# Scores of two differential heads as one group of four row groups in a fused two-layer transformer trunk

## The chip, the cores and the metric

One Trainium2 chip, one of its cores. The metric is the device time of one execution in microseconds (us). TensorE (PE in the rows) multiplies matrices, its weight loads stand in rows of their own (PEld), VectorE is DVE, ScalarE is ACT, GpSimd is POOL, and SyncE (SP) issues the loads of weights. Each engine works through its own queue of instructions in order, and engines wait for each other at semaphores.

## The reference

Two layers over 256 tokens of width 1024, all in float32. A layer normalizes x, makes queries, keys and values for 16 heads of width 64 with one projection, runs three kinds of attention side by side, projects back, adds attention over a memory, and ends with a gated feed-forward part. The change touches the four *differential* heads. Each has two softmaxes with queries and keys of width 32 and one set of values:

```
s1 = q1 @ k1.T * 32**-0.5          # 256 x 256, causal mask
s2 = q2 @ k2.T * 32**-0.5
p  = softmax(s1) - lam * softmax(s2)
o  = p @ v
```

The other twelve heads (six with a dilated mask, six causal) have one softmax each, with queries and keys of width 64. So a layer has 20 softmaxes, numbered n = 0 to 19: 0 to 7 belong to the differential heads (two to a head), 8 to 19 to the others.

## The kernel before

**Float32 as three products.** A weight unit (128 x 2048) is loaded into `raw`, ACT rounds it into `whi` (`split_hi`, L636 or L638) and DVE takes the difference into `wlo` (`split_lo`, L961 or L963). TensorE multiplies hi by hi, hi by lo and lo by hi. Units go round a ring of three buffers, and SP loads the next unit of a buffer when both splits of the last one are done. Units 0 to 11 of a layer are the q/k/v projection, 12 and 13 the key/value projection of the memory (`mkv`).

**Places.** In the first half of a layer all engines follow one counter g, the *place*. At each place TensorE runs one *filler*: four 512-column matmuls of the projections (L1581), which need nothing from the attention. The attention is put between the fillers by tables at the end of the file: what stands at place g in a table is issued ahead of filler g by TensorE, and at place g in the order of the loops by ACT (L773 to L824) and DVE (L1245 to L1292). The order of every queue is fixed by these tables; nothing is decided at run time.

**One pair of softmaxes** (`duo` d, softmaxes 2d and 2d+1) goes through these steps:

- `score(d)` on TensorE (L1702 to L1711): for the two halves of the queries, one matmul per softmax. A differential softmax uses 32 rows of the array (rows 0, 32, 64 or 96 upwards, as `SOFTMAXES` gives it); the two matmuls of a pair use different rows and write to different PSUM banks (`n % 2`, so banks 0 and 1). It waits until the maxima of the previous pair are taken, since those read the same banks.
- `mask_max(n)` on DVE (L1163 to L1180): adds the mask, writes the scores from PSUM to one of four buffers `prob`, and takes the row maxima (`nm`).
- `exps(n)` on ACT (L728 to L735), then `combine(h)` on DVE (L1182 to L1193), which puts the two softmaxes of differential head h together.
- `transpose_p(m)` on TensorE (L1713 to L1731), `probT_out(m)` on ACT (L737 to L741), `weigh_v(m)` on TensorE (L1733 to L1747), the product with the values.

**The second half of the keys.** `transpose_qk(2)` on TensorE (L1658 to L1675) transposes the keys of heads 8 to 15 into banks 3 and 4. ACT copies bank 3 (`qkT_out(2)`, L720) and DVE copies bank 4 (`qkT_out(2)`, L1159) into `kT`. Since `weigh_v(0)` writes its results into banks 3 and 4 too, it waits for both copies (`qkT_first` and `qkT_second`, L1737 and L1738).

**The other waits that matter here.** `split_lo` of a unit waits for its `split_hi`; `chunk_out(i, t)` on ACT (L687 to L697) takes a finished projection block out of PSUM.

Of the kernel before, what the change touches and what calls it, by code (L numbers as in the profile page):

```python
# [42 lines left out]
DIFF, DIL, MOBA = 4, 6, 6  # L43
# [34 lines left out]
NS = len(SOFTMAXES)  # L78
# [22 lines left out]
def trunk(nc, x, mem, w, gains, consts, out):  # L101
    with ExitStack() as ctx:
# [25 lines left out]
        prob = [sq[:, 512 * b:512 * b + 512] for b in range(4)]  # L128
# [36 lines left out]
        masks = table[:, 0:6 * P].rearrange("p (c n) -> p c n", c=2)  # L165
# [34 lines left out]
        ps = ctx.enter_context(nc.psum_tensor("ps", [P, 8, 512], F32))  # L200
# [72 lines left out]
        scores = signal("scores", DUOS)  # L273
        nmax = signal("nmax", NS)
# [335 lines left out]
        def _(act):  # L610
# [58 lines left out]
            for layer in range(DEPTH):  # L669
# [38 lines left out]
                def qkT_out(e):  # L708

                    act.wait_ge(qkT_ps.sem, qkT_ps.at(layer, 2 * e + 1))  # L710
                    dst, j = (kT, qT)[e % 2], 4 * (e // 2)
                    bank = QKT_BANKS[e][0]
                    if e % 2:
# [9 lines left out]
                    if layer == 0 and e == 1:  # L723
                        act.wait_ge(qkT_ps.sem, qkT_ps.at(layer, 2 * e + 2))
                        act.activation(qT[:, 2:4, :].rearrange("p k n -> p (k n)"), ps[:, QKT_BANKS[1][1], :], ACT.Copy)\
                           .then_inc(qkT_second.sem, 1)
# [46 lines left out]
                for g in range(6, LAST + 1):  # L773
# [10 lines left out]
                    for m in range(HEADS):  # L784
                        if g == T_AT[m]:
                            probT_out(m)
                    for e in range(4):
                        if g == QKT_AT[e]:
                            qkT_out(e)
                    for d in range(DUOS):  # L790
                        for b in range(2):
                            if g == S_AT[d] + EXPS_AFTER[d][b]:
                                exps(2 * d + b)
# [151 lines left out]
        def _(dve):  # L945
# [116 lines left out]
            for layer in range(DEPTH):  # L1062

                if layer == 0:
# [5 lines left out]
                    for k in range(4):  # L1070
# [7 lines left out]
                        ins = dve.tensor_tensor(wlo[0][:, cols], raw[0][:, cols], whi[0][:, cols].bitcast(F32), ALU.subtract)  # L1078
# [84 lines left out]
                def mask_max(n):  # L1163

                    head, _, rows = SOFTMAXES[n]
                    kind = 1 if DIFF <= head < DIFF + DIL else 0
                    if n % 2 == 0:
                        dve.wait_ge(scores.sem, scores.at(layer, n // 2 + 1))
                    if layer == n == 0:
                        dve.wait_ge(s_table.sem, 16)  # L1170
                        dve.wait_ge(s_memss.sem, 1)
                    if n >= 4:

                        dve.wait_ge(pT_ps.sem, pT_ps.at(layer, SOFTMAXES[n - 4][0] + 1))
                    for t, (a, b) in enumerate(((0, P), (P, 3 * P))):
                        scale = -float(rows) ** -0.5 if kind else q_root[:, t, n:n + 1]
                        ins = dve.tensor_tensor_reduce(prob[n % 4][:, a:b], ps[:, n % 2, a:b], masks[:, kind, a:b],  # L1177
                                                       scale, -3.0 * NEG, ALU.add, ALU.min,
                                                       nm[:, n, t:t + 1])
                    ins.then_inc(nmax.sem, 1)  # L1180
# [64 lines left out]
                for g in range(6, LAST + 1):  # L1245
# [3 lines left out]
                    for d in range(DUOS):  # L1249
                        if g == S_AT[d]:  # L1250
                            mask_max(2 * d)
                            mask_max(2 * d + 1)
                        if d < DIFF and g == S_AT[d] + COMBINE_AFTER[d]:
                            combine(d)
                    for e in range(4):
                        if g == QKT_DVE_AT[layer][e]:
                            qkT_out(e)
# [149 lines left out]
                for t in range(T):  # L1407
                    ins = dve.tensor_scalar(rs_diag[:, t * P:(t + 1) * P], ident, rs[:, 1, t:t + 1], None, ALU.mult)
# [83 lines left out]
        def _(pe):  # L1492
# [50 lines left out]
            for layer in range(DEPTH):  # L1543
# [114 lines left out]
                def transpose_qk(e):  # L1658

                    if e % 2:  # L1660
                        pe.wait_ge(roped.sem, roped.at(layer, e // 2 + 1))
                    else:
                        pe.wait_ge(roped_keys.sem, roped_keys.at(layer, e // 2 + 1))
                    part, half = 1 - e % 2, e // 2
                    if layer == 0 and e < 2:
                        pe.wait_ge(m_lo.sem, (2, 4)[e])
                    for b in range(2):
                        if e == 3 and b == 0:
                            pe.wait_ge(nmax.sem, nmax.at(layer, 2 * HALF_DUO))
                        for j in range(2):  # L1670
                            for t in range(T):
                                a = j * SEQ + t * P
                                c = part * D + (4 * half + 2 * b + j) * P
                                ins = pe.transpose(ps[:, QKT_BANKS[e][b], a:a + P], qkv[:, t, c:c + P], ident)
                        ins.then_inc(qkT_ps.sem, 1)  # L1675
# [23 lines left out]
                                           mem_sb[:, t, (4 * h + k) * P:(4 * h + k + 1) * P], ident)  # L1699
                    ins.then_inc(m_ps.sem, 1)  # L1700

                def score(d):  # L1702

                    if d:
                        pe.wait_ge(nmax.sem, nmax.at(layer, 2 * d))
                    for qa, qb, kb, a in ((0, P, P, 0), (P, 2 * P, 2 * P, P)):
                        for n in (2 * d, 2 * d + 1):
                            h, base, rows = SOFTMAXES[n]
                            q, k = qT[base:base + rows, h // 2, qa:qb], kT[base:base + rows, h // 2, 0:kb]
                            ins = pe.matmul(ps[:, n % 2, a:a + kb], q, k, start=True, stop=True)  # L1710
                    ins.then_inc(scores.sem, 1)  # L1711

                def transpose_p(m):  # L1713
                    n = 2 * m if m < DIFF else m + DIFF
# [56 lines left out]
                for g in range(LAST + 1):  # L1771
                    for n in range(2, 4):
                        if layer == 0 and g == FIRST_AT[n - 2]:
                            build_x(0, X_MIX, FIRST_ORDER[n])
                    if layer and g == 3:
                        for q in range(2, 4):
                            build_x(layer, X_MIX, q)
                    for q in range(4):
                        if layer == 0 and g == MEM_AT[q]:
                            build_mem(q)  # L1780
                    for m in range(DIFF):
                        if g == V_AT[m]:
                            weigh_v(m)
                    for m in range(DIFF, HEADS, 2):
                        if g == V_AT[m + 1]:
                            weigh_v_duo(m)
                    for d in range(DUOS):
                        if g == SCORES_AT[d]:
                            if d == 0:
                                pe.wait_ge(qkT_first.sem, qkT_first.at(layer, 2))  # L1790
                                pe.wait_ge(qkT_second.sem, qkT_second.at(layer, 2))
                            if d == HALF_DUO:
                                pe.wait_ge(qkT_first.sem, qkT_first.at(layer, 4))
                                pe.wait_ge(qkT_second.sem, qkT_second.at(layer, 4))
                            score(d)
                    for m in range(HEADS):
                        if g == T_AT[m]:
                            transpose_p(m)
                    for e in range(4):
                        if g == QKT_AT[e]:  # L1800
                            transpose_qk(e)
                    for e in range(N_BUILD):
                        if g == HB_AT[e]:
                            build_heads(e)
                    if g < FILLERS:
                        filler(g)
                    elif g < FILLERS + 3 * len(OUT1_EARLY):
                        (c, t), part = OUT1_EARLY[(g - FILLERS) // 3], (g - FILLERS) % 3
                        out1_half(c, t, part, 0)

                for c in range(2):
                    for part in range(3):
                        ins = out1_half(c, 0, part, 1)
# [3 lines left out]
                for j in range(2):  # L1817
                    for t in range(T):
                        a = j * SEQ + t * P
                        ins = pe.transpose(ps[:, 3, a:a + P], kvm[:, t, j * P:(j + 1) * P], ident)  # L1820
# [233 lines left out]
LO_AT[0][9 - 3], LO_AT[0][10 - 3] = 46, 50  # L2054
HI_AT = [[6 * (u - 2) for u in range(3, U_MQ)] for _ in range(DEPTH)]
HI_AT[0][9 - 3] = 44
QKT_DVE_AT = ((27, None, 61, 71), (32, 43, 61, 71))
QKT_AT = (32, 43, 61, 71)
COMBINE_AFTER = (4, 2, 4, 4)
S_AT = (45, 47, 54, 61, 66, 69, 73, 77, 82, 86)  # L2060
SCORES_AT = (45, 47, 54, 61, 66, 69, 73, 77, 81, 86)
EXPS_AFTER = ((1, 2), (1, 1), (1, 2), (1, 2), (1, 2), (1, 2), (1, 2), (1, 1), (2, 2), (1, 2))
T_AT = (54, 61, 66, 69, 71, 73, 77, 77, 79, 79, 84, 84, 90, 90, 92, 92)
V_AT = (66, 69, 69, 71, 77, 77, 79, 79, 81, 81, 86, 86, 92, 92, 97, 97)
V_CHUNKS = (4, 5)
SUMS = [(0, 0, 0), (0, 0, 1), (1, 0, 0), (1, 0, 1), (1, 1, 0), (2, 0, 0), (2, 0, 1), (2, 1, 0)]
# [23 lines left out]
PT_BANKS = (2, 2, 2, 2, 2, 2, 2, 3, 2, 3, 2, 4, 2, 4, 2, 1)  # L2090
H_CHUNKS = (0, 2, 4, 6)
QKT_BANKS = ((0, 1), (3, 4), (3, 4), (0, 1))


DVE_LO = U_MQ
# [126 lines left out]
```

## Time and profile before

| | |
|---|---|
| Runs | 691.69, 691.01, 691.58 us; median 691.58 us |
| Profiled execution | 691.29 us, with a span of 689.5 us |
| TensorE busy | 680.8 us of the span |
| VectorE busy | 500.5 us |
| ScalarE busy | 394.2 us |
| GpSimd busy | 107.3 us |

A row of the timeline gives the start in us from the span's start, the time from the first start to the last end, the engine, the line, the operation, what it writes and reads, the shape, and how many equal instructions were merged. Matmuls are pipelined, so the end of one lies behind the start of the next: what a group costs is read from the start of one group to the start of the next. A float32 matmul stands as two instructions. A square bracket gives the time that the engine stood idle before the row and who ended that.

### The profile page before, as it was taken

Reading aid. Unit: us, or ns where it says so; the run is one execution under the profiler, and the core shown is the slowest. Engines: PE = TensorE matmul, PEld = TensorE weight load, DVE = VectorE, ACT = ScalarE, POOL = GpSimd, SP = SyncE. Lnnn points to the kernel's source line nnn. Section 1 sums busy time; section 2 is a strip of 40 time slices with the busy share of each in tenths; the row PEclk is TensorE's granted clock in tenths of the full one; section 3 lists DMA queues with packets and bytes.
Section 4 is the critical chain, followed back from the end, with each engine's and each line's share of the span. In section 5 each row is a group of like instructions: output and inputs, shape, how many; then the busy total and the mean of one; then the engine's idle time right before and its main releaser. Section 6 shows DMA issues by size and latency. Waiting matters only on the chain.

```text
span 689.5 us, 10761 instructions
## 1 busy us (share of the span) xinstructions
PE 680.8 (99%) x3782; PEld 568.2 (82%) x3782; DVE 500.5 (73%) x960; ACT 394.2 (57%) x648; POOL 107.3 (16%) x125
## 2 busy tenths in 40 slices
PE   9999999999999999999999999999999999999998
PEld 7887877778888888888888778778798888888886
DVE  5798887586766666666678798875877666666665
ACT  6977776478444444444566668664775444444442
POOL 6254020227000000000034230202530000000000
PEclk9999999999999999999999999999999999999999
DMA  9945532146666666666547525214366666666631
GB/s 324 331 140 178 181 123 61 63 123 181 184 185 183 183 183 183 186 186 190 203 149 245 200 104 184 92 31 125 99 204 182 193 196 193 195 193 186 184 122 62
DMA packets 121248, 115.65 MB, mean 168 GB/s; under 512 B 2688, under 2 KB 95104, under 8 KB 121216
## 3 DMA queue, kind: packets, MB, share of 16 engines
q1 hardware_dynamic: 120640, 114.31, 53.5%
q10 hardware_dynamic: 576, 0.93, 0.4%
q8 instruction: 19, 0.31, 0.2%
q14 instruction: 13, 0.11, 0.0%
HBM read 114.17 MB, written 1.05 MB: 167 GB/s over the span
## 4 chain that ended last, share of the span: by engine, by line
PE 88%; ACT 5%; DVE 3%; issue 2%; DMA 1%; SPq 0%; ACTq 0%; DVEq 0%
PE ps L1968 21%; PE ps L1581 19%; PE ps L1973 11%; PE ps L2016 6%; PE ps L2017 6%; PE ps L2018 6%; PE ps L1995 3%; PE ps L1652 3%; PE ps L1710 2%; PE ps L1902 2%; PE ps L1730 2%; ACT sq L855 1%; DVE wlo L961 1%; PE ps L1501 1%; PE ps L1766 1%
## 5 line engine op out<-in xcount | busy, mean ns | idle before, releaser
L961 DVE TENSOR_TENSOR wlo<-raw,whi 128x2048 fp32r<-128x2048 f32 (+1 forms) x95 | 211.8, 2246 | 44.6 <-ACT whi L636 42.4
L636 ACT ACTIVATE whi<-raw 128x2048 fp32r<-128x2048 f32 (+1 forms) x102 | 188.7, 1875 | 11.7 <-PE ps L2018 6.5
L1968 PE MATMUL ps<-both,whi 128*128 128x512 f32 x640 | 159.2, 391 | 0.0
L1968 PEld LDWEIGHTS ps<-both,whi 128*128 128x128 f32 x640 | 117.6, 188 | 22.8
L1581 PE MATMUL ps<-whi,both 128*128 128x512 f32 x384 | 99.4, 396 | 0.5 <-ACT both L648 0.5
L1973 PEld LDWEIGHTS ps<-both,wlo 128*128 128x128 f32 x640 | 87.3, 190 | 6.2
L899 ACT ACTIVATE qkv<-ps 128x512 f32<-128x512 f32 x42 | 25.1, 598 | 112.7 <-PE ps L1973 112.7
L1973 PE MATMUL ps<-both,wlo 128*128 128x256 f32 x640 | 89.2, 282 | 0.0
L1581 PEld LDWEIGHTS ps<-whi,both 128*128 128x128 f32 x384 | 70.5, 188 | 16.3 <-issue 1.7
L2016 PE MATMUL ps<-whi,ahi 128*128 128x512 f32 x176 | 69.1, 393 | 0.0
L2017 PE MATMUL ps<-wlo,ahi 128*128 128x512 f32 x176 | 69.0, 392 | 0.0
L2018 PE MATMUL ps<-whi,alo 128*128 128x512 f32 x176 | 68.5, 389 | 0.0
L1423 DVE TENSOR_TENSOR qkv<-ps,qkv 128x512 f32<-128x512 f32 x42 | 28.9, 689 | 45.8 <-ACT qkv L899 45.7
L506 POOL TENSOR_TENSOR wlo<-raw,whi 128x2048 fp32r<-128x2048 f32 x7 | 32.1, 4601 | 183.5 <-DVE wlo L1477 179.0
L907 ACT ACTIVATE qkv<-qkv 128x256 f32<-128x256 f32 x44 | 18.4, 418 | 65.4 <-DVE qkv L1428 65.4
L1581 PE MATMUL ps<-wlo,both 128*128 128x512 f32 x192 | 52.3, 395 | 0.1
L732 ACT ACTIVATE sq<-sq,nm 128x128 f32<-128x128 f32 x80 | 35.4, 447 | 16.0 <-DVE nm L1177 15.8
L1581 PEld LDWEIGHTS ps<-wlo,both 128*128 128x128 f32 x192 | 35.4, 188 | 7.8 <-DVE wlo L961 0.7
L648 ACT ACTIVATE both<-ps,starter 128x128 fp32r<-128x128 f32 x96 | 26.6, 379 | 21.7 <-PE ps L1501 21.7
L2018 PEld LDWEIGHTS ps<-whi,alo 128*128 128x128 f32 x176 | 33.1, 188 | 7.2
L2016 PEld LDWEIGHTS ps<-whi,ahi 128*128 128x128 f32 x176 | 33.2, 189 | 5.7
L2017 PEld LDWEIGHTS ps<-wlo,ahi 128*128 128x128 f32 x176 | 33.2, 189 | 5.3
(211 smaller groups left out, 907.3 us busy)
## 6 DMA issues: line engine op xcount, KB each, us to landing
raw<-in_w_gate_up SPq DMA_DIRECT2D x88, 512.0 KB, 5.0
raw<-in_w_in SPq DMA_DIRECT2D x23, 1024.0 KB, 5.4
raw<-in_w_down SPq DMA_DIRECT2D x22, 1024.0 KB, 4.9
raw<-in_w_out SPq DMA_DIRECT2D x8, 1024.0 KB, 5.0
raw<-in_w_mkv SPq DMA_DIRECT2D x4, 1024.0 KB, 5.4
raw<-in_w_mq SPq DMA_DIRECT2D x4, 512.0 KB, 3.5
raw<-in_w_mo SPq DMA_DIRECT2D x2, 1024.0 KB, 4.8
xs<-in_x SPq DMA_DIRECT2D x4, 256.0 KB, 5.2
```

What stands on the lines that cost most here:

```text
L506: pool.tensor_tensor(wlo[s][:, 0:n], raw[s][:, 0:n], whi[s][:, 0:n].bitcast(F32), ALU.subtract)\
L636: ins = act.activation(whi[s][:, cols], raw[s][:, cols], ACT.Copy)
L648: ins = act.activation(thi[:, c, tok], ps[:, X_BANKS[b][q], k * P:(k + 1) * P], ACT.Copy, scale=gain)
L732: ins = act.activation(prob[n % 4][:, a:b], prob[n % 4][:, a:b], ACT.Exp, bias=nm[:, n, t:t + 1], scale=-1.0, accum_out=zs[:, n, t:t + 1])
L961: ins = dve.tensor_tensor(wlo[s][:, cols], raw[s][:, cols], hi, ALU.subtract)
L1423: dve.tensor_tensor(gu[b], gu_banks(b, 0), small_gu[b], ALU.add).then_inc(gu_done.sem, 1)
L1581: ins = pe.matmul(ps[:, acc, :], x_part[:, k0 + k, t * P:(t + 1) * P], w_part[s][:, 512 * k:512 * k + 512], start=first and k == 0 and par ...
L1968: pe.matmul(ps[:, bank, :], whi[s][:, a:a + P], both[:, :, k, :], start=(k == 0), stop=False)
L1973: ins = pe.matmul(ps[:, bank, 0:256], wlo[s][:, a:a + P], thi[:, k, :], start=False, stop=(k == KC - 1))
L2016: pe.matmul(acc, ahi[b][:, tok], whi[s][:, a:a + 512], start=first, stop=False)
L2017: pe.matmul(acc, ahi[b][:, tok], wlo[s][:, a:a + 512], start=False, stop=False)
L2018: ins = pe.matmul(acc, alo[b][:, tok], whi[s][:, a:a + 512], start=False, stop=last)
```

## The change

`score` takes the pairs of two differential heads at once: its loop runs over four softmaxes, in four row groups, and writes to four banks (`SCORE_BANKS`: 0, 1, 3, 4 for softmaxes 0 to 3 and again for 4 to 7; later ones keep 0 and 1). It is called for d = 0 and d = 2 among the differential pairs, at places 45 and 54; the calls at 47 and 61 are gone. Because softmaxes 4 to 7 now use banks 3 and 4 as well, `transpose_qk(2)` waits until the maxima of all eight differential softmaxes are taken. The `scores` semaphore still goes up once per pair.

The tables move what follows: the maxima of pair 1 from place 47 to 46 and of pair 3 from 61 to 57 (with their `exps`, which follow at fixed distances), `transpose_p(1)` from 61 to 57, `transpose_qk(2)` and both copies into `kT` from 61 to 63. `combine(3)` moves from 65 to 61 and the others stay.

```diff
-                        ins = dve.tensor_tensor_reduce(prob[n % 4][:, a:b], ps[:, n % 2, a:b], masks[:, kind, a:b],
+                        ins = dve.tensor_tensor_reduce(prob[n % 4][:, a:b], ps[:, SCORE_BANKS[n], a:b], masks[:, kind, a:b],
...
                     for b in range(2):
+                        if e == 2 and b == 0:
+                            pe.wait_ge(nmax.sem, nmax.at(layer, 2 * DIFF))
                         if e == 3 and b == 0:
                             pe.wait_ge(nmax.sem, nmax.at(layer, 2 * HALF_DUO))
...
-                def score(d):
+                def score(d, duos):
                     if d:
                         pe.wait_ge(nmax.sem, nmax.at(layer, 2 * d))
                     for qa, qb, kb, a in ((0, P, P, 0), (P, 2 * P, 2 * P, P)):
-                        for n in (2 * d, 2 * d + 1):
+                        for n in range(2 * d, 2 * d + 2 * duos):
                             h, base, rows = SOFTMAXES[n]
                             q, k = qT[base:base + rows, h // 2, qa:qb], kT[base:base + rows, h // 2, 0:kb]
-                            ins = pe.matmul(ps[:, n % 2, a:a + kb], q, k, start=True, stop=True)
-                    ins.then_inc(scores.sem, 1)
+                            ins = pe.matmul(ps[:, SCORE_BANKS[n], a:a + kb], q, k, start=True, stop=True)
+                            if a and n % 2:
+                                ins.then_inc(scores.sem, 1)
...
-                        if g == SCORES_AT[d]:
+                        if g == SCORES_AT[d] and (d >= DIFF or d % 2 == 0):
...
-                            score(d)
+                            score(d, 2 if d < DIFF else 1)
...
-QKT_DVE_AT = ((27, None, 61, 71), (32, 43, 61, 71))
+QKT_DVE_AT = ((27, None, 63, 71), (32, 43, 63, 71))
...
-S_AT = (45, 47, 54, 61, 66, 69, 73, 77, 82, 86)
+S_AT = (45, 46, 54, 57, 66, 69, 73, 77, 82, 86)
...
+SCORE_BANKS = 2 * (0, 1, 3, 4) + (NS - 8) // 2 * (0, 1)
```

ACT's queue from place 57 to place 64. L732 is `exps`, L696 `chunk_out`, L638 `split_hi` of unit 12, L741 `probT_out(1)`, L720 the copy into `kT`. Before:

```order
L696 ACTIVATE qkv<-ps,rs 128x512 x2
L638 ACTIVATE whi<-raw,starter 128x512 x4
L741 ACTIVATE probT<-ps 128x384
L720 ACTIVATE kT<-ps,k_col 128x256 x2
L732 ACTIVATE sq,zs<-sq,nm 128x128
```

The same stretch now:

```order
L696 ACTIVATE qkv<-ps,rs 128x512
L741 ACTIVATE probT<-ps 128x384
L732 ACTIVATE sq,zs<-sq,nm 128x128
L732 ACTIVATE sq,zs<-sq,nm 128x256
L732 ACTIVATE sq,zs<-sq,nm 128x128
L732 ACTIVATE sq,zs<-sq,nm 128x256
L696 ACTIVATE qkv<-ps,rs 128x512
L638 ACTIVATE whi<-raw,starter 128x512 x4
L720 ACTIVATE kT<-ps,k_col 128x256 x2
```

The exponentials of softmaxes 6 and 7 moved from behind the split of unit 12 and the copy of `kT` to a place ahead of both.

DVE's queue over the same places. L1177 is `mask_max` (of softmaxes 6 and 7 here), L1186 the first instruction of `combine`, L1159 the copy into `kT`, L963 `split_lo` of unit 12. Before:

```order
L961 TENSOR_TENSOR wlo<-raw,whi 128x2048 [waits hi_done2]
L1186 RECIPROCAL lam_z<-zs 128x2 [waits probs]
...
L1177 ISA sq,nm<-ps,table,q_root 128x128 [waits pT_ps,scores]
...
L1159 TENSOR_SCALAR kT<-ps,k_col 128x512 [waits qkT_ps]
L963 SCALAR_TENSOR_TENSOR wlo<-raw,starter,whi 128x512 [waits hi_done0]
L963 SCALAR_TENSOR_TENSOR wlo<-raw,starter,whi 128x512 x3
L1186 RECIPROCAL lam_z<-zs 128x2 [waits probs]
```

Now:

```order
L961 TENSOR_TENSOR wlo<-raw,whi 128x2048 [waits hi_done2]
L1177 ISA sq,nm<-ps,table,q_root 128x128 [waits pT_ps,scores]
...
L1186 RECIPROCAL lam_z<-zs 128x2 [waits probs]
...
L963 SCALAR_TENSOR_TENSOR wlo<-raw,starter,whi 128x512 [waits hi_done0]
L963 SCALAR_TENSOR_TENSOR wlo<-raw,starter,whi 128x512 x3
L1159 TENSOR_SCALAR kT<-ps,k_col 128x512 [waits qkT_ps]
```

The maxima of 6 and 7 moved ahead of both `combine`s, and the copy of `kT` moved behind both `combine`s and behind the four instructions that split unit 12.

TensorE's queue at places 61 to 66. L1710 (now L1713) is `score`, L1730 `transpose_p(1)`, L1674 (now L1676) `transpose_qk(2)`, L1744 (now L1748) the first matmul of `weigh_v(0)`. Before:

```order
L1710 MATMUL ps<-kT,qT 128x128 [waits nmax]
...
L1730 MATMUL ps<-starter,sq 128x128 [waits pT_out,combined]
L1730 MATMUL ps<-starter,sq 128x128 x2
L1674 MATMUL ps<-starter,qkv 128x128 [waits roped_keys]
L1674 MATMUL ps<-starter,qkv 128x128 x7
L1581 MATMUL ps<-wlo,both 128x512 [waits lo_done1]
...
L1744 MATMUL ps<-qkv,probT 128x64 [waits qkT_second,proj_out,qkT_first,pT_out]
```

Now, from place 62 on:

```order
L1581 MATMUL ps<-whi,both 128x512 x4
L1676 MATMUL ps<-starter,qkv 128x128 [waits nmax,roped_keys]
L1676 MATMUL ps<-starter,qkv 128x128 x7
L1581 MATMUL ps<-whi,both 128x512 [waits hi_done1,proj_out]
...
L1748 MATMUL ps<-qkv,probT 128x64 [waits qkT_second,proj_out,qkT_first,pT_out]
```

The score is gone from place 61, the transposes of the keys stand two fillers later and wait for `nmax`, and three fillers in place of five lie between them and `weigh_v(0)`, which waits as before.

## Rows read from the trace of the kernel before

**Rows 1.** Page, part 1 (busy us) and part 2 (granted clock, 40 slices, tenths).

```profile
PE 680.8 (99%) x3782; PEld 568.2 (82%) x3782; DVE 500.5 (73%) x960; ACT 394.2 (57%) x648; POOL 107.3 (16%) x125
...
PEclk9999999999999999999999999999999999999999
```

**Rows 2.** Timeline of TensorE, layer 1, around the score at place 47.

```profile
394.68 1.09 PE L1581 MATMUL ps<-wlo,both 128*128 128x512 f32 x4
395.70 0.92 PE L1710 MATMUL ps<-kT,qT 32*128 32x128 f32 x8
396.56 2.12 PE L1581 MATMUL ps<-whi,both 128*128 128x512 f32 x8
398.51 1.07 PE L1581 MATMUL ps<-wlo,both 128*128 128x512 f32 x4
```

**Rows 3.** Timeline of TensorE, layer 0: score at place 47, weigh_v at 66.

```profile
57.59 0.92 PE L1710 MATMUL ps<-kT,qT 32*128 32x128 f32 x8 [0.56 <-DVE nm L1177]
...
79.42 0.33 PE L1744 MATMUL ps<-qkv,probT 128*128 128x64 f32 x2
```

**Rows 4.** Timeline of TensorE, layer 1, places 59 to 66.

```profile
408.95 1.98 PE L1581 MATMUL ps<-whi,both 128*128 128x512 f32 x8
410.93 0.92 PE L1710 MATMUL ps<-kT,qT 32*128 32x128 f32 x8
411.78 0.55 PE L1730 MATMUL ps<-starter,sq 128*128 128x128 f32 x3
412.17 1.04 PE L1674 MATMUL ps<-starter,qkv 128*128 128x128 f32 x8
412.96 1.17 PE L1581 MATMUL ps<-wlo,both 128*128 128x512 f32 x4
413.96 1.99 PE L1581 MATMUL ps<-whi,both 128*128 128x512 f32 x8
415.79 1.07 PE L1581 MATMUL ps<-wlo,both 128*128 128x512 f32 x4
...
417.60 0.33 PE L1744 MATMUL ps<-qkv,probT 128*128 128x64 f32 x2
```

**Rows 5.** Timeline of DVE, layer 1, places 54 to 61.

```profile
409.44 0.34 DVE L1177 CUSTOM_DVE_ANT_0 sq<-ps,table,q_root 128x128 f32<-128x128 f32 x1
...
410.79 2.29 DVE L961 TENSOR_TENSOR wlo<-raw,whi 128x2048 fp32r<-128x2048 f32 x1
413.00 0.16 DVE L1186 RECIPROCAL lam_z<-zs 128x2 f32<-128x2 f32 x1
...
415.46 0.75 DVE L1159 TENSOR_SCALAR kT<-ps,k_col 128x512 f32<-128x512 f32 x1
416.12 2.73 DVE L963 SCALAR_TENSOR_TENSOR wlo<-raw,starter,whi 128x512 fp32r<-128x512 f32 x4
```

**Rows 6.** Timeline of ACT, layer 1, places 55 to 61.

```profile
410.23 0.40 ACT L732 ACTIVATE sq<-sq,nm 128x128 f32<-128x128 f32 x1 [3.36 <-DVE nm L1177]
...
412.00 1.24 ACT L696 ACTIVATE qkv<-ps,rs 128x512 f32<-128x512 f32 x2
413.14 2.56 ACT L638 ACTIVATE whi<-raw,starter 128x512 fp32r<-128x512 f32 x4
...
415.97 0.82 ACT L720 ACTIVATE kT<-ps,k_col 128x256 f32<-128x256 f32 x2
```

**Rows 7.** Timeline of DVE, layer 0, places 50 and 58.

```profile
65.11 2.44 DVE L961 TENSOR_TENSOR wlo<-raw,whi 128x2048 fp32r<-128x2048 f32 x1 [0.42 <-ACT whi L636]
...
74.74 0.16 DVE L1186 RECIPROCAL lam_z<-zs 128x2 f32<-128x2 f32 x1
```

**Rows 8.** Windows behind the last matmul: length, busy times (x count), then PEclk.

```profile
686.20:688.70 2.50, 0.00 (x0) 0.00 (x0) 0.77 (x2) 0.00 (x0) 0.00 (x0) 1.00 0.96 363
688.80:689.50 0.70, 0.00 (x0) 0.00 (x0) 0.00 (x0) 0.00 (x0) 0.00 (x0) 0.50 0.00 0
```

**Rows 9.** Timeline of TensorE, the program's first matmuls.

```profile
1.08 3.78 PE L1538 MATMUL ps<-ones 128*128 128x128 f32 x16 [1.08 <-DVE ones L1060]
```

More of the change, by code:

```diff
@@ L2056 @@
 HI_AT[0][9 - 3] = 44
-QKT_DVE_AT = ((27, None, 61, 71), (32, 43, 61, 71))
-QKT_AT = (32, 43, 61, 71)
-COMBINE_AFTER = (4, 2, 4, 4)
-S_AT = (45, 47, 54, 61, 66, 69, 73, 77, 82, 86)
-SCORES_AT = (45, 47, 54, 61, 66, 69, 73, 77, 81, 86)
+QKT_DVE_AT = ((27, None, 63, 71), (32, 43, 63, 71))
+QKT_AT = (32, 43, 63, 71)
+COMBINE_AFTER = (4, 3, 4, 4)
+S_AT = (45, 46, 54, 57, 66, 69, 73, 77, 82, 86)
+SCORES_AT = (45, 45, 54, 54, 66, 69, 73, 77, 81, 86)
 EXPS_AFTER = ((1, 2), (1, 1), (1, 2), (1, 2), (1, 2), (1, 2), (1, 2), (1, 1), (2, 2), (1, 2))
-T_AT = (54, 61, 66, 69, 71, 73, 77, 77, 79, 79, 84, 84, 90, 90, 92, 92)
+T_AT = (54, 57, 66, 69, 71, 73, 77, 77, 79, 79, 84, 84, 90, 90, 92, 92)
 V_AT = (66, 69, 69, 71, 77, 77, 79, 79, 81, 81, 86, 86, 92, 92, 97, 97)
```

## The prediction

> **What bounds the kernel now.** The first part of the page comes first: TensorE is busy for 680.8 of 689.5 us [rows 1]. So a stretch without work on TensorE moves the end, and so does work taken off it, as long as the other engines still deliver in time. Whether they do is a matter of one stretch per layer, places 45 to 66, so I read the timelines of TensorE, DVE and ACT there, layer 1 first. The reader is to see that TensorE runs its fillers nearly without a break (eight take 413.96 to 415.79, 1.83 us, so four take 0.92) [rows 4], while DVE goes from one piece to the next without idle time: maxima of 4 and 5 at 409.44, a split at 410.79, `combine(2)` at 413.00, the copy of `kT` at 415.46, the split of unit 12 at 416.12 [rows 5]. ACT waits 3.36 us for DVE's maxima before the exponentials of 4 and 5 [rows 6]. In this stretch the attention is paced by DVE, and TensorE hides that with fillers.
>
> **What the removed groups cost.** Score 1 in layer 1: from the four fillers at 394.68 to the next at 396.56 are 1.88 us, 0.96 more than four fillers need; the eight behind it take 1.95 (to 398.51), 0.12 more than 1.83 [rows 2]. Together 1.08. Score 3: the eight fillers ahead take 1.98 (0.15 more), the group itself 410.93 to 411.78, 0.85 [rows 4]. Together 1.00. Layer 0 has the same two, and in score 1 also 0.56 us of idle time behind the maxima [rows 3]. In all 2 x 2.08 + 0.56 = 4.7 us of TensorE time are taken out.
>
> **What the two groups of four cost.** No row shows four. The nearest row is a group of two in 0.85 us. At best four take the same 0.85; at worst the second two run behind the first, 1.70. I take the best, since the two of a pair already overlap in these rows; which end holds does not enter the sum, because TensorE waits at place 63 (below) for longer than the two possible extras before it, 2 x 0.85 = 1.7 us.
>
> The Trainium skill's "TensorE: Matmul & The Clock Gate" (Part 3, Measured speedup vs the span model) gives 3.07 times for four row tiles of 32 rows, so as an estimate a group of four would take 0.85 x 4 / 3.07 = 1.1 us, inside these ends; no run here shows it yet. The page "TensorEngine Tiling (Array Packing)" (PSUM Bottleneck) speaks against the change: packing speeds up TensorE but not the reading of PSUM, which may then bound. By the first rule alone the kernel would gain 4.7 - 4 x 0.25 = 3.7 us, by the second nothing; the rows of DVE side with the second.
>
> **Place 63, the new wait (layer 1).** The maxima of 6 and 7 can start when DVE reaches them: now right behind the split that ends at 413.00, where `combine(2)` stood. A pair of maxima takes 1.35 us (409.44 to 410.79) [rows 5], so all eight are done at 414.35. TensorE gets to `transpose_qk(2)` early. Filler 61 started at 412.96; taking off the two scores (1.08 and 1.00) and the transposes ahead of it (412.17 to 412.96, 0.79) it starts at 410.09 (`transpose_p(1)` only moves from 61 to 57, still ahead). Two fillers later it is 411.9, and TensorE waits 2.4 us until 414.4. Transposes (0.79) and three fillers (2.75) later it is at `weigh_v(0)` at 417.9, against 417.60 before [rows 4]. The gain is gone here already. Nothing else is queued on TensorE that another engine needs sooner than the transposes.
>
> **Place 66, the wait that decides.** `weigh_v(0)` needs both copies into `kT`. ACT's copy stands behind the exponentials of 6 and 7, a `chunk_out` and the split of unit 12; DVE's copy stands behind the difference of that same unit. So this becomes one chain, each step with its row:
> - maxima of 6 and 7 start: 413.00 [rows 5]
> - exponentials start 0.79 behind the maxima (409.44 to 410.23) [rows 5, 6]: 413.79
> - two softmaxes take 410.23 to 412.00, 1.77 [rows 6]: 415.56
> - one `chunk_out`, half of 412.00 to 413.14, 0.57: 416.13
> - `whi` of unit 12, 2.56: 418.69
> - `wlo` of unit 12 on DVE, 2.73 [rows 5]: 421.42
> - the copy into `kT`, 0.75: 422.17
>
> `combine(3)` fits beside it: it needs the exponentials (415.56), and a `combine` takes 415.46 - 413.00 less 1.35 for a pair of maxima, 1.1 us, so DVE is free again long before 418.69. ACT's own copy (0.82 behind 418.69) is earlier than DVE's. So `weigh_v(0)` starts at 422.17 and not at 417.60: 4.57 us late, of which TensorE stands still about 4.2.
>
> Layer 0 has the same queues. `combine(2)` stood at 74.74 [rows 7]. On DVE the maxima of 2 and 3 now stand ahead of a split, so ACT gets to their exponentials, and to the split of its own behind them, earlier; I take DVE's idle 0.42 in front of its split [rows 7] as gone, so the chain starts at 74.32, ends 9.17 later at 83.49, and `weigh_v(0)` moves from 79.42 [rows 3] by 4.07 (4.49 if the 0.42 stays).
>
> Behind the copy DVE holds the maxima of 8 and 9, whose score comes after `weigh_v(0)` on TensorE anyway; behind ACT's copy stands `probT_out(2)`, which also waits for TensorE. SP's load into the buffer of unit 12 waits for `wlo`, which now ends at 421.42 and before at about 418.85, 2.6 us later while TensorE is 4.6 later, so the loads gain slack. POOL is not passed. From there all queues are those of before and TensorE has no idle time that could take the delay back.
>
> Sum against the profiled execution: 691.29 + 4.57 + 4.07 = 699.9; the runs' median is 0.3 above that execution, so 700.2.
>
> **TensorE's clock.** Before, the granted clock is full in every slice of the program [rows 1]. After the last matmul it was still full up to 688.7 and at half (1.2 of 2.4 GHz) from 688.8 on, with TensorE idle since 686.2 [rows 8]. The stalls here are longer (4.2 us, and 2.4 us shortly ahead), and the longest within the rows above, 0.56, did no harm. So I expect the clock to have fallen when TensorE resumes, in each layer. The price: nothing if it does not fall, and at most what the first matmuls show, 16 of 128 columns in 3.78 us (0.24 each, where eight transposes of this size take 0.79, 0.10 each) [rows 9, 4]: 3.78 us at half the clock lose 1.9. Part of the slow time may lie inside the stall; I take 1.1 per layer, 2.2 in all. Forecast: 702.4.
>
> The Trainium skill ("TensorE: Matmul & The Clock Gate", HAM oscillation) has the same rule, that gaps between bursts of matmuls put the clock back to half; the rows of the program's end agree.
>
> **Rivals.** *The clock holds.* Same stalls, 700.2. For it: no gap inside the program ever cost the clock. Against it: the fall at the end came after only 2.6 us.
>
> *The work taken out shows: faster.* 691.6 - 4.7 = 686.9, or up to 1.7 us later in each layer if four do not overlap. One point decides, at place 66: TensorE would get there at 417.60 - 2.08 = 415.5, so `kT` would have to be copied by then, and the maxima of 6 and 7 would have to start 9.2 us earlier, at 406.3. For it: 99% busy TensorE. Against it: DVE has no idle time before 413.00 to get there from [rows 5].
>
> *Only place 63 counts.* If the split of unit 12 did not have to wait for the exponentials, TensorE would stand at `weigh_v(0)` 0.3 us late in each layer, less slack elsewhere: 691.6 +/- 0.6, no change. Against it is the order on ACT, where the split stands behind them.
>
> *Four groups do not overlap.* Then the change does not do what it says, but its 1.7 us lie inside the wait at place 63: the time of the forecast.
>
> **How the numbers follow.** Stalls and a lower clock 58%, stalls with full clock 28%, faster 8%, only place 63 6%. About 0.2% (1.4 us) is what a measurement of this kernel can tell from no change. Slower 0.87, within 0.2% 0.05, faster 0.08. The range: 700.2 less 1.4 (0.7 a layer, an allowance for steps of DVE and ACT that take another time than in these rows), and 702.4 plus the rest of the clock's bound (2 x 0.8) and 1 for the same steps: 698.8 to 705.0; it leaves out the two lower cases and little above.
>
> **What would show it.** In the profile after: `transpose_qk(2)` with about 2.4 us of idle time ended by DVE's maxima, the first matmul of `weigh_v(0)` with about 4 us ended by DVE's copy into `kT`, in both layers; DVE idle before L963, ended by ACT's L638; a granted clock below 1 behind 83 and 422 us if the clock falls. A group of four in 0.85 to 1.1 us. The prediction is wrong if `weigh_v(0)` starts without waiting.

## The result and the profile after

The changed kernel takes 703.71 us (median of 5 runs, 702.49 to 704.98) against 691.59 us before (5 runs on the same chip, 691.01 to 691.69). The ratio is 1.0178, 95% interval 1.0166 to 1.0190: slower by 1.8%. The forecast was 702.4 in a range of 698.8 to 705.0.

The page of the changed kernel: the span, busy times of the engines, the slices of TensorE and of its granted clock. Against [rows 1], TensorE is busy for 0.7 us less and the span is 12.4 us longer: TensorE stands idle for 701.9 - 680.1 = 21.8 us, before for 8.7.

```profile
span 701.9 us, 10763 instructions
PE 680.1 (97%) x3782; PEld 568.4 (81%) x3782; DVE 500.8 (71%) x960; ACT 394.1 (56%) x648; POOL 107.5 (15%) x125
PE   8999699999999999999999987999999999999998
PEclk9999999999999999999999999999999999999999
```

Where it stands idle is in TensorE's timeline. The code has moved: `score` is now L1713, `transpose_p` L1734, `transpose_qk` L1676, `weigh_v` L1748 to L1750. Layer 0 first, from the first group of four on:

```profile
53.81 0.94 PE L1713 MATMUL ps<-kT,qT 32*128 32x128 f32 x16
54.68 1.20 PE L1581 MATMUL ps<-whi,both 128*128 128x512 f32 x4
...
76.04 1.07 PE L1676 MATMUL ps<-starter,qkv 128*128 128x128 f32 x8 [3.00 <-DVE nm L1177]
...
83.84 0.41 PE L1748 MATMUL ps<-qkv,probT 128*128 128x64 f32 x2 [3.96 <-DVE kT L1159]
...
84.71 1.65 PE L1713 MATMUL ps<-kT,qT 64*128 64x128 f32 x8
...
86.85 1.64 PE L1581 MATMUL ps<-whi,both 128*128 128x512 f32 x4
88.33 1.07 PE L1581 MATMUL ps<-wlo,both 128*128 128x512 f32 x4
...
420.62 1.06 PE L1676 MATMUL ps<-starter,qkv 128*128 128x128 f32 x8 [2.55 <-DVE nm L1177]
...
428.41 0.41 PE L1748 MATMUL ps<-qkv,probT 128*128 128x64 f32 x2 [3.98 <-DVE kT L1159]
```

The group of four takes 54.68 - 53.81 = 0.87 us, where two took 0.85 [rows 4]. Two new waits stand in each layer: at the transposes of place 63 (3.00 and 2.55 us, ended by DVE's maxima) and at `weigh_v(0)` of place 66 (3.96 and 3.98 us, ended by DVE's copy into `kT`). `weigh_v(0)` starts at 83.84, before at 79.42 [rows 3]. Behind it a block of four fillers takes 88.33 - 86.85 = 1.48 us, where four took 0.92 [rows 4].

DVE in layer 1, from the maxima of softmax 6 to the copy into `kT` (L1186 is `combine(2)` and `combine(3)`; before, [rows 5]):

```profile
419.03 0.35 DVE L1177 CUSTOM_DVE_ANT_0 sq<-ps,table,q_root 128x128 f32<-128x128 f32 x1
...
420.38 0.16 DVE L1186 RECIPROCAL lam_z<-zs 128x2 f32<-128x2 f32 x1
...
421.73 0.17 DVE L1186 RECIPROCAL lam_z<-zs 128x2 f32<-128x2 f32 x1
...
424.75 2.74 DVE L963 SCALAR_TENSOR_TENSOR wlo<-raw,starter,whi 128x512 fp32r<-128x512 f32 x4 [1.82 <-ACT whi L638]
427.41 0.75 DVE L1159 TENSOR_SCALAR kT<-ps,k_col 128x512 f32<-128x512 f32 x1
```

ACT over the same stretch (before, [rows 6]): exponentials of softmax 6, `chunk_out`, split of unit 12, its own copy into `kT`.

```profile
419.83 0.40 ACT L732 ACTIVATE sq<-sq,nm 128x128 f32<-128x128 f32 x1 [0.74 <-DVE nm L1177]
...
421.60 0.67 ACT L696 ACTIVATE qkv<-ps,rs 128x512 f32<-128x512 f32 x1
422.17 2.55 ACT L638 ACTIVATE whi<-raw,starter 128x512 fp32r<-128x512 f32 x4
424.62 0.82 ACT L720 ACTIVATE kT<-ps,k_col 128x256 f32<-128x256 f32 x2
```

Read across the two fences, this is one chain: maxima 419.03, exponentials 419.83, `chunk_out` 421.60, `whi` 422.17, `wlo` 424.75, copy 427.41, `weigh_v(0)` 428.41. Apart from the maxima of 7, which run beside the exponentials of 6, no step overlaps the next by more than 0.1 us, and DVE stands idle for 1.82 us inside the chain.

The windows show the clock that the page's slices hide: length, busy time of each engine, then the granted clock.

```profile
54.00:84.46 30.46, 23.50 (x136) 18.47 (x134) 25.95 (x77) 18.89 (x48) 8.89 (x17) 1.00 0.41 138
84.46:87.88 3.42, 3.42 (x17) 2.46 (x16) 0.54 (x3) 0.65 (x2) 0.00 (x0) 0.50 0.80 307
...
429.20:432.62 3.42, 3.42 (x15) 2.57 (x15) 0.80 (x7) 0.91 (x2) 0.00 (x0) 0.50 0.80 302
```

Behind each wait at place 66 the clock stands at half (1.2 of 2.4 GHz) while TensorE is fully busy.

### The profile page after: what moved, and what is told of

It is laid out like the page before. It is cut to its first block, busy times and chain, and to the rows that moved or that the text cites. A ratio compares the mean times of both kernels' runs of the same rounds, so it can differ in the third digit from the quotient of the medians.

```text
span 701.9 us, 10763 instructions
## 1 busy us (share of the span) xinstructions
PE 680.1 (97%) x3782; PEld 568.4 (81%) x3782; DVE 500.8 (71%) x960; ACT 394.1 (56%) x648; POOL 107.5 (15%) x125
## 4 chain that ended last, share of the span: by engine, by line
PE 82%; DVE 9%; ACT 6%; issue 2%; DMA 1%; SPq 0%; POOL 0%; ACTq 0%; DVEq 0%; POOLq 0%
PE ps L1972 21%; PE ps L1581 15%; PE ps L1977 11%; PE ps L2020 6%; PE ps L2021 6%; PE ps L2022 6%; PE ps L1999 3%; PE ps L1652 3%; DVE wlo L961 3%; ACT sq L732 2%; PE ps L1906 2%; PE ps L1501 1%; PE ps L1713 1%; DVE sq L1177 1%; ACT sq L855 1%
## 5 line engine op out<-in xcount | busy, mean ns | idle before, releaser
L1581 PE MATMUL ps<-whi,both 128*128 128x512 f32 x384 | 101.1, 399 | 0.6 <-ACT both L648 0.6
L732 ACT ACTIVATE sq<-sq,nm 128x128 f32<-128x128 f32 x80 | 35.4, 446 | 20.7 <-DVE nm L1177 20.6
```

Source lines behind the costliest of these rows:

```text
L732: ins = act.activation(prob[n % 4][:, a:b], prob[n % 4][:, a:b], ACT.Exp, bias=nm[:, n, t:t + 1], scale=-1.0, accum_out=zs[:, n, t:t + 1])
L1581: ins = pe.matmul(ps[:, acc, :], x_part[:, k0 + k, t * P:(t + 1) * P], w_part[s][:, 512 * k:512 * k + 512], start=first and k == 0 and par ...
```

## The experiments

| Kernel | Median us (range, runs) | Ratio to before (95%) |
|---|---|---|
| changed kernel | 703.71 (702.49 to 704.98, 5) | 1.0178 (1.0166 to 1.0190) |
| e8: no wait at place 63 | 705.91 (704.67 to 706.37, 4) | 1.0214 (1.0197 to 1.0231) |
| e2: the new queue order with pairs | 706.42 (704.71 to 706.81, 4) | 1.0215 (1.0200 to 1.0231) |
| e7: DVE's difference of unit 12 behind its copy | 695.41 (695.16 to 695.61, 4) | 1.0060 (1.0045 to 1.0075) |
| e1: unit 12 behind both copies | 695.01 (693.99 to 695.78, 4) | 1.0051 (1.0036 to 1.0067) |
| e4: idle matmuls at place 66, too many | 711.49 (710.36 to 711.63, 4) | 1.0290 (1.0274 to 1.0305) |
| e6: idle matmuls in both waits | 700.61 (700.47 to 700.73, 4) | 1.0134 (1.0118 to 1.0149) |
| e3: keys in banks 0 and 1, queue mended | 688.89 (688.70 to 689.10, 6) | 0.9967 (0.9955 to 0.9979) |
| e5: e3 with unit 13 moved | 688.83 (688.61 to 689.16, 5) | 0.9964 (0.9950 to 0.9977) |

The kernel before took 691.16 to 691.30 us (medians of 7 to 10 runs) beside them.

**Does place 66 decide, or do the two waits add up (e8)?** The second half of the keys goes to banks 0 and 1, so that place 63 no longer waits for the maxima of 6 and 7; every place in the tables stays.

```diff
-                            pe.wait_ge(nmax.sem, nmax.at(layer, 2 * DIFF))
+                            pe.wait_ge(nmax.sem, nmax.at(layer, 2 * DIFF - 2))
...
                     if m == 0:
+                        pe.wait_ge(nmax.sem, nmax.at(layer, 2 * DIFF))
...
-QKT_BANKS = ((0, 1), (3, 4), (3, 4), (0, 1))
+QKT_BANKS = ((0, 1), (3, 4), (0, 1), (0, 1))
```

> The changed kernel without its wait at place 63: the second half of the keys is transposed into banks 0 and 1, so the transposes wait only for the maxima of softmaxes 4 and 5, and weigh_v(0) waits for the maxima of 6 and 7 beside the copies into kT. All tables stay, so the chain on ACT and DVE (maxima of 6 and 7, exponentials, unit 12's split and difference, copy) is that of the changed kernel. My theory, as in the prediction: the chain decides at place 66, so TensorE waits there for the sum of both waits (about 7 us in layer 0, 6.5 in layer 1) and the time is that of the changed kernel, 703.7 us (702.0 to 705.0; one stretch of idle time per layer may cost the clock more or less than two). Rival: the two waits add up independently, and without the first the kernel is faster by its 3.00 and 2.55 us: 698.2.

It took 705.91. TensorE's timeline, `weigh_v(0)` of the two layers (L1749 here):

```profile
83.84 0.66 PE L1749 MATMUL ps<-qkv,probT 128*128 128x64 f32 x2 [6.57 <-DVE kT L1159]
...
429.00 0.66 PE L1749 MATMUL ps<-qkv,probT 128*128 128x64 f32 x2 [6.61 <-DVE kT L1159]
```

In layer 0 it starts at 83.84, to the hundredth where the changed kernel has it: the idle time has only moved from place 63 to place 66. So the chain on ACT and DVE decides, and the wait at place 63 costs nothing of its own. The rival's 698.2 falls. In layer 1 `weigh_v(0)` comes 0.59 us later than in the changed kernel. My range was missed by 0.9 us at its upper end, on the clock's side. The windows show that it was at half for longer, with 4.57 us of matmuls in the stretch of layer 0 and 4.15 in that of layer 1. Half of these is 4.4 us lost, 0.9 more than the same half of the changed kernel's two stretches (3.4), and this execution took 704.67, 1.0 more.

```profile
81.59:88.41 6.82, 4.57 (x19) 3.65 (x20) 2.49 (x7) 0.61 (x2) 0.00 (x0) 0.50 0.45 154
...
426.34:433.15 6.81, 4.15 (x18) 3.32 (x19) 2.48 (x5) 0.18 (x1) 0.00 (x0) 0.50 0.46 156
```

**Is it the group of four, or the order that came with it (e2)?** The queue order of the changed kernel, with pairs in banks 0 and 1 in place of groups of four (the lines that set the banks are left out).

```diff
-                        if e == 2 and b == 0:
-                            pe.wait_ge(nmax.sem, nmax.at(layer, 2 * DIFF))
...
-                            score(d, 2 if d < DIFF else 1)
+                            score(d, 1)
...
-SCORES_AT = (45, 45, 54, 54, 66, 69, 73, 77, 81, 86)
+SCORES_AT = (45, 47, 54, 57, 66, 69, 73, 77, 81, 86)
```

> The changed order of all queues, but scores in pairs as before: banks 0 and 1, at places 45, 47, 54 and 57, and no wait for the maxima ahead of the transposes of the keys. Queue theory: as slow as the changed kernel, weigh_v(0) waits for the same chain, 702 to 706 us. Group theory: the cost is gone, 691 to 693 us.

It took 706.42, no less than the changed kernel: in this order the loss does not need the group of four. The test is not clean, though, because pairs that share banks 0 and 1 bring a wait of their own, and the granted clock is at half for 6.8 us in each layer. The idle time stands mostly at another place: in TensorE's timeline the score of softmaxes 6 and 7 (L1711) waits for the maxima of 4 and 5, and `weigh_v(0)` only for what is left.

```profile
73.54 1.65 PE L1711 MATMUL ps<-kT,qT 32*128 32x128 f32 x8 [4.38 <-DVE nm L1177]
...
87.32 0.41 PE L1746 MATMUL ps<-qkv,probT 128*128 128x64 f32 x2 [0.52 <-DVE kT L1159]
```

**Is the split of unit 12 the link (e7, e1)?** e7 moves only DVE's difference behind its copy; e1 moves the split and the difference behind both copies.

```diff
+for row in LO_AT:          # e7
+    row[12 - 3] = 64
...
+for table in (HI_AT, LO_AT):          # e1
+    for row in table:
+        row[12 - 3] = 64
```

> The changed kernel with one move: DVE takes the difference of unit 12 behind its copy into kT (place 64 in place of 63); ACT's order stays. My theory: weigh_v(0) waits for a chain that ends with ACT's split, DVE's difference (2.74) and DVE's copy. Without the difference in it the chain ends with ACT's copy, at 424.62 + 0.82 = 425.4 us in layer 1 in place of 428.4: 3.0 us earlier in each layer, 697.7 us, and up to 1.6 us less in each layer if the clock then holds (694.5). Rival: ACT's order alone decides, since ACT's own copy stands behind the split as well and TensorE's clock or loads fill what is gained: 702 to 704.

e7 took 695.41, below the 697.7 that I put first. In its timeline of TensorE, layer 1, `weigh_v(0)` waits 1.10 us, 2.9 less than in the changed kernel; the profile names no releaser:

```profile
421.40 0.41 PE L1748 MATMUL ps<-qkv,probT 128*128 128x64 f32 x2 [1.10 <-issue]
```

ACT's timeline has the last thing that it needs, ACT's copy, which ends at 421.30:

```profile
420.49 0.81 ACT L720 ACTIVATE kT<-ps,k_col 128x256 f32<-128x256 f32 x2
```

So ACT's order leaves only this rest, and the rival (702 to 704) falls. What else is gained is the clock: in layer 0 it fell earlier, behind place 63, and its slow fillers ran where TensorE would have waited for the copy; in layer 1 it did not fall. The windows:

```profile
77.13:80.55 3.42, 3.42 (x9) 2.63 (x8) 2.19 (x6) 3.42 (x7) 0.00 (x0) 0.50 0.57 221
...
417.00:421.00 4.00, 3.29 (x17) 2.46 (x15) 2.64 (x8) 4.00 (x10) 0.00 (x0) 1.00 0.63 245
```

This is the profiled execution, the fastest of the four (695.16, mean granted clock 0.998). The other three had 0.995 and took only 0.2 to 0.45 us longer.

> The changed kernel with the split of unit 12 moved behind both copies into kT, on ACT and on DVE; the groups of four, their banks and the wait at place 63 stay. Queue theory (the copy of kT stood behind the exponentials and the split): weigh_v(0) no longer waits, 4.1 us come back in each layer, and the clock may or may not fall in the wait at place 63 that stays (2.5 to 3.0 us): 692.3 to 695.5 us. Group theory (the groups of four with their shared banks are what costs): no change worth naming, 702 to 704 us.

e1 took 695.01. `weigh_v(0)` no longer waits, but place 63 still does, in TensorE's timeline:

```profile
76.31 1.94 PE L1676 MATMUL ps<-starter,qkv 128*128 128x128 f32 x8 [2.97 <-DVE nm L1177]
...
416.69 1.25 PE L1676 MATMUL ps<-starter,qkv 128*128 128x128 f32 x8 [2.54 <-DVE nm L1177]
```

and by the windows the clock fell behind that wait:

```profile
76.12:79.52 3.40, 3.21 (x12) 2.95 (x13) 2.89 (x11) 3.40 (x11) 0.00 (x0) 0.50 0.79 302
...
417.45:420.86 3.41, 3.41 (x11) 2.74 (x10) 2.01 (x6) 3.41 (x9) 0.00 (x0) 0.50 0.66 256
```

What is left adds up: 691.2 - 4.7 (the score groups) + 2.97 + 2.54 (the waits) + 3.3 (half of the 3.21 and 3.41 us of matmuls at half clock) = 695.3; this execution took 695.64. The two executions with a mean granted clock of 0.997 and 0.998 were 1.25 to 1.8 us shorter than the two with 0.995. So in e1, where no wait stands behind the slow fillers, the lower clock seems to show in the time, and in e7, where one does, hardly. Only the profiled executions have windows, so how often the clock fell in the others is not shown.

**What does the clock cost (e4, e6)?** Both put matmuls into the waits whose results nothing uses. e4 puts 36 ahead of `weigh_v(0)`:

```diff
                         if g == V_AT[m]:
+                            if m == 0:
+                                warm_up(36, 0)
                             weigh_v(m)
```

> The changed kernel with 36 idle matmuls of 128 columns into a free bank ahead of weigh_v(0), which fill the wait there with about 3.8 us of work and change no result. If the lower clock after the wait is caused by TensorE standing idle there, the clock stays full behind it and 1.6 us come back in each layer: 700.5 us. If the wait at place 63 alone brings the clock down, or the clock is no cost, it stays at 703 to 704 us.

e4 took 711.49 and tells nothing on the price. The 36 float32 matmuls stand as 72 instructions and took 8.2 us, about twice the wait that they were to fill, and its mean clock is 0.994 to 0.998 in all four runs, so it fell as well. In the profiled execution it fell behind place 63 (0.51 from 77.13 to 80.54 us and from 425.30 to 428.71), where the changed kernel, with the same queues up to there and the same wait of 3.00 us, kept it full.

```profile
81.23 8.20 PE L1538 MATMUL ps<-ones 128*128 128x128 f32 x72
89.27 0.33 PE L1748 MATMUL ps<-qkv,probT 128*128 128x64 f32 x2
```

e6 uses that measured size and fills both waits, except that 1.15 and 0.72 us of idle time stay at place 63, ahead of its idle matmuls and ended by ACT's `chunk_out`:

```diff
+                            if m == 0:
+                                warm_up(17, 0)
                             weigh_v(m)
...
+                            if e == 2:
+                                pe.wait_ge(proj_out.sem, proj_out.at(layer, 9))
+                                warm_up(8, 5)
                             transpose_qk(e)
```

> The changed kernel, with idle matmuls in TensorE's two waits of each layer: 8 at place 63 and 17 at place 66 (0.22 us each by the run before, so 1.8 and 3.8 us), both a little shorter than the waits. They compute nothing that is used. My theory: the slow stretch of 3.41 us behind place 66 comes from the idle time and costs 1.6 us in each layer; with TensorE at work the granted clock stays at 1.0 and the time is 703.7 - 2 x 1.6 = 700.5 us (700.0 to 701.2). Rival: the time is made by the chain of DVE and ACT alone, and the fillers behind the slow stretch only take up time that would be lost anyway: 703.7 with or without the slow stretch.

e6 took 700.61. `weigh_v(0)` starts at 83.94, 0.10 later than in the changed kernel, so the chain is as long as before; but the granted clock is 1.0 in all of its runs, and the fillers behind it start at 85.88 and 86.90, where the changed kernel has 86.85 and 88.33. The rival's 703.7 falls:

```profile
79.81 3.96 PE L1538 MATMUL ps<-ones 128*128 128x128 f32 x34
83.94 0.41 PE L1748 MATMUL ps<-qkv,probT 128*128 128x64 f32 x2 [0.17 <-issue]
...
84.72 0.93 PE L1713 MATMUL ps<-kT,qT 64*128 64x128 f32 x8
...
85.88 1.18 PE L1581 MATMUL ps<-whi,both 128*128 128x512 f32 x4
86.90 1.08 PE L1581 MATMUL ps<-wlo,both 128*128 128x512 f32 x4
```

The clock therefore costs 703.71 - 700.61 = 3.1 us, 1.55 per layer, in the profiled execution of the changed kernel (703.71, mean clock 0.995). It is not a fixed price: another of its runs, with 0.988, took 703.73. With the lower clock the spread goes too: e6's runs lie within 0.26 us, those of the changed kernel within 2.5.

**A version that keeps the group of four (e3, e5).** e3 takes both waits away: the bank change of e8, DVE's copy at place 60 (the transposes and ACT's copy stay at 63), unit 12's split behind the copies, and the exponentials of 6 and 7 behind ACT's copy. `weigh_v(0)` waits for the maxima alone, and `score(4)` for the copies.

```diff
...
-                        pe.wait_ge(qkT_first.sem, qkT_first.at(layer, 3 if V_CHUNKS[0] == 4 else 2))
-                        pe.wait_ge(qkT_second.sem, qkT_second.at(layer, 3 if V_CHUNKS[0] == 4 else 2))
+                        pe.wait_ge(nmax.sem, nmax.at(layer, 2 * DIFF))
...
-QKT_DVE_AT = ((27, None, 63, 71), (32, 43, 63, 71))
+for row in HI_AT:
+    row[12 - 3] = 64
+for row in LO_AT:
+    row[12 - 3] = 66
+QKT_DVE_AT = ((27, None, 60, 71), (32, 43, 60, 71))
...
-EXPS_AFTER = ((1, 2), (1, 1), (1, 2), (1, 2), (1, 2), (1, 2), (1, 2), (1, 1), (2, 2), (1, 2))
+EXPS_AFTER = ((1, 2), (1, 1), (1, 2), (6, 6), (1, 2), (1, 2), (1, 2), (1, 1), (2, 2), (1, 2))
...
-QKT_BANKS = ((0, 1), (3, 4), (3, 4), (0, 1))
+QKT_BANKS = ((0, 1), (3, 4), (0, 1), (0, 1))
```

> Groups of four, with the second half of the keys transposed into banks 0 and 1 (waiting for the maxima of 4 and 5 only; score 4 waits for the copies of kT, weigh_v(0) for all eight maxima), the copies of kT ahead of the split of unit 12, and that split after the exponentials of 6 and 7. Queue theory: neither place 63 nor place 66 holds TensorE any more, and the 4.7 us that the groups take out show, less what DVE cannot follow later: 687 to 689 us. Group theory: above 698 us, the groups are still there.

e3 took 688.89, 0.33% faster than the kernel before (interval 0.21 to 0.45%). The waits of places 63 and 66 are gone. The run makes these moves together, so it shows that they suffice with the groups of four kept, not which of them are needed. In TensorE's timeline smaller ones are left, one behind ACT and two where DVE comes late with the divide of the next heads:

```profile
74.52 1.19 PE L1581 MATMUL ps<-whi,both 128*128 128x512 f32 x4 [0.25 <-ACT qkv L696]
...
87.97 0.55 PE L1734 MATMUL ps<-starter,sq 128*128 128x128 f32 x3 [0.62 <-DVE sq L1220]
...
425.00 0.55 PE L1734 MATMUL ps<-starter,sq 128*128 128x128 f32 x3 [0.64 <-DVE sq L1220]
```

e5 tries to remove these by moving the split of unit 13 behind the maxima of 10 and 11:

```diff
-    row[12 - 3] = 64
+    row[12 - 3], row[13 - 3] = 64, 69
...
-    row[12 - 3] = 66
+    row[12 - 3], row[13 - 3] = 66, 71
```

(and the exponentials of softmax 5 one place later, behind a `chunk_out`; those of 4 stay.)

> This is the version with the groups of four in which the keys' transposes use banks 0 and 1 (e3_banks, 688.89), and in addition DVE takes the maxima of softmaxes 10 and 11 ahead of the split of unit 13 (split at places 69 and 71), and the exponentials of 4 and 5 stand one place later, behind a chunk_out. My theory: what e3_banks still lost were two waits of TensorE, 0.64 us per layer at the transposes that wait for DVE's divide, and about 0.3 us in layer 0 at a filler that waits for chunk_out. If both go, 688.9 - 2 x 0.64 - 0.3 = 687.3 us (687.0 to 687.8), close to the 686.9 that taking out 4.7 us of TensorE time would give. Rival: the wait only moves to the next step of DVE, since DVE's work is the same in sum: 688.9, no change against e3_banks.

e5 took 688.83, the same as e3: the rival was right. The old waits are gone and others stand in TensorE's timeline, 0.48 us in layer 0 and then 0.33 + 0.18 and 0.34 + 0.18 (three of the five rows below): 1.5 us in all, as in e3.

```profile
78.17 0.93 PE L1713 MATMUL ps<-kT,qT 64*128 64x128 f32 x8 [0.48 <-issue]
...
438.61 0.55 PE L1734 MATMUL ps<-starter,sq 128*128 128x128 f32 x3 [0.34 <-DVE sq L1220]
...
441.18 0.87 PE L1769 MATMUL ps<-probT,qkv 128*64 128x256 f32 x8 [0.18 <-ACT probT L741]
```

## Why the prediction was right, point by point

- **The removed groups, 4.7 us.** Nearly held. With both waits gone, e3 keeps 2.3 us of it (691.16 - 688.89); 1.5 stand as waits in its trace, 0.25 + 0.62 + 0.64. From the start of the first score to `weigh_v(0)` its TensorE takes 23.23 and 22.84 us in the two layers (before 25.34 and 24.82); with the 0.25 us of waiting inside the first added back, the groups gave 4.3 and not 4.7. The last 0.5 of the sum is not traced.
- **A group of four, 0.85 to 1.70.** 0.87: four overlap as two do, and the rival of no overlap falls. The estimate from the Trainium skill's "TensorE: Matmul & The Clock Gate" (Part 3, Measured speedup vs the span model) was 1.1 us; the rows decide, 0.87. The Trainium skill's "TensorEngine Tiling (Array Packing)" (PSUM Bottleneck) warns that reading PSUM may then bound; no run here shows that by itself, since what is left in e3 waits mostly for DVE's divide of later heads (L1220).
- **Place 63, 2.4 us in layer 1.** 2.55, and by e8 it does not enter the sum, as the prediction had it.
- **Place 66, the chain.** Each link held: 0.80 to the exponentials (0.79 forecast), 1.77 for them, 0.57, 2.58 to the difference (2.56), 2.66 to the copy (2.73). From the start of the copy to `weigh_v(0)` it is 1.00, not 0.75: the 0.25 from the copy's end to the first matmul was left out. So the chain is 9.38 and not 9.17 long.
- **How late `weigh_v(0)` is.** Layer 0: 83.84 - 79.42 = 4.42 (forecast 4.07, or 4.49 if DVE's 0.42 us idle time stayed; the chain began at 74.46 and not at 74.32). Layer 1: the chain began 419.03 - 413.00 = 6.03 later than DVE got there before, `weigh_v(0)` came 428.41 - 417.60 = 10.81 later, so this layer adds 4.78 (forecast 4.57).
- **The clock.** It fell in both layers, as forecast; the rows did not force that, and the prediction gave it 58 against 28%. The term was mis-sized: 1.1 per layer forecast, 1.55 measured by e6; the assumption that part of the slow time lies inside the stall did not hold, since TensorE was busy through all of it. The term's upper bound, 1.9, came from the program's first matmuls taken as running at half the clock; the windows of the kernel before give 1.00 there (0.90 to 6.10 us), so the profile does not show it. Their 0.24 us per instruction against 0.11 at full clock in e4 (8.04 us for 72) speaks for it. The clock fell behind both waits at place 66, so the trace agrees as to the direction with the rule that the prediction cites from the Trainium skill ("TensorE: Matmul & The Clock Gate", HAM oscillation); at which waits the clock falls the runs leave open (below).

With these sizes the sum closes: 691.29 + 4.42 + 4.78 + 2 x 1.55 = 703.6, measured 703.71. All three terms had been forecast too small, so errors that cancel did not help the forecast. Of the rivals, "the clock holds" is e6 (forecast 700.2, measured 700.61 with the waits filled), and "the work taken out shows" is approached only by e3, where the chain was taken off the path.

## What to carry to other kernels

Ask of a merged step what now has to be finished before the step can begin or its buffers be reused, and follow that through every queue: here 4.7 us of work left TensorE, and a chain across ACT and DVE that had lain beside the fillers came onto the path for 9.2 us. An edit of banks, waits and tables (what stands ahead of a copy) decided the sign, 703.7 or 688.9, and not the group of four itself. On an engine that has been busy all along, a stall of some microseconds can cost more than its length: here 1.55 us more in each layer for the lower clock, and less where the slow work ran into a further wait (e7).

## What the runs showed of the hardware that was not expected

- The length of a wait alone does not tell whether the clock falls: the wait of place 63 in layer 0 (3.00 us in the changed kernel, 2.97 in e1) was followed by full clock in the one and by half in the other, and in layer 1 the wait of about 2.55 us by half in e1 and by full clock in e7. In e4 the same 3.00 us as in the changed kernel were followed by half. What decides stays open.
- Eight float32 matmuls of 32 rows (sixteen instructions) in four row groups take as long as four in two, 0.87 against 0.85 us.
- A float32 matmul of 128 columns against the same 128 rows, back to back, takes 0.22 us at full clock (8.04 us for 36 in e4, granted clock 1.00), so idle matmuls have to be counted from a trace before they are used to fill a wait.
